# A layer pair with expert lookup: 40 instead of 20 of 64 gate batches beside the u tiles, and their work spread over the engines

## What is computed

```
top_v, top_i = top_k(sub_scores, 16)               # two halves, 128 keys each
cand = top_v[0, :, None] + top_v[1, None, :]       # 256 pairs
best_v, best_pos = top_k(cand, 16)
expert = (top_i[0] * 128 + top_i[1]) at best_pos
gates = softmax(best_v)
hid = gelu(u[expert] . h) * gates                  # 8 x 16 = 128 experts a token
out = sum over the 128 experts of hid * v[expert]
```

## Time and profile before

| | |
|---|---|
| median of the runs | 2865.11 us |
| profiled execution: span | 2863.0 us |
| own time of the profiled execution | not given apart; the runs are 2865.05, 2865.11 and 2867.16 us, so 2.1 us or a little more lie around the span |
| TensorE busy | 2716.7 us (95%) |
| VectorE | 1595.0 us (56%) |
| ScalarE | 937.4 us (33%) |
| GpSimd | 1362.7 us (48%) |
| DMA moved | 598.85 MB, mean 209 GB/s |

### The profile page before, as it was taken

One profiled execution on the slowest core, in us unless ns is written; L12 is line 12 of the kernel. 1 busy time (PEld: TensorE's weight loads), 2 busy tenths in 40 slices (PEclk: granted clock), 3 DMA queues, 4 the chain that ended last, 5 costly groups with the idle time before them and its releaser, 6 DMA issues.

```text
span 2863.0 us, 32244 instructions
## 1 busy us (share of the span) xinstructions
PE 2716.7 (95%) x12062; PEld 2057.0 (72%) x12062; DVE 1595.0 (56%) x3064; ACT 937.4 (33%) x1684; POOL 1362.7 (48%) x1004
## 2 busy tenths in 40 slices
PE   8989999998999899999998789999999999999996
PEld 7856888776888678888777678888888864444442
DVE  1033044476314343440224757999999999756667
ACT  3275343655424333222334433111113670000001
POOL 4432444566446234444352436645446664645445
PEclk9999999999999999999999899999999999999999
DMA  5321233332244136663331035999999849999998
GB/s 164 104 58 30 74 105 92 113 102 70 102 141 145 53 93 194 206 185 123 78 105 38 30 110 205 377 409 408 409 409 385 318 146 409 409 411 409 410 409 327
DMA packets 219373, 598.85 MB, mean 209 GB/s; under 512 B 22337, under 2 KB 47314, under 8 KB 218834
## 3 DMA queue, kind: packets, MB, share of 16 engines
q1 hardware_dynamic: 135280, 300.70, 30.7%
q0 software_dynamic: 75968, 275.81, 24.9%
q10 hardware_dynamic: 7970, 20.28, 2.2%
HBM read 584.84 MB, written 7.41 MB: 207 GB/s over the span
## 4 chain that ended last, share of the span: by engine, by line
PE 72%; DMA 11%; DVE 9%; POOL 3%; ACT 2%; issue 2%; POOLq 0%; DVEq 0%; ACTq 0%; SPq 0%
PE ps L1893 14%; PE ps L1373 14%; PE ps L1374 13%; PE ps L1375 13%; DMA rows<-in_v,expert 6%; DMA rows<-in_u,expert 5%; DVE ps L2597 2%; PE ps L1882 2%; DVE rows L2583 2%; PE ps L1339 1%; POOL wlo L1148 1%; PE ps L1912 1%; PE ps L1472 1%; POOL rows L1279 1%; PE ps L1559 1%
## 5 line engine op out<-in xcount | busy, mean ns | idle before, releaser
L1148 POOL TENSOR_TENSOR wlo<-wraw,whi 128x1024 fp32r<-128x1024 f32 x258 | 627.3, 2442 | 799.5 <-ACT whi L614 709.8
L614 ACT ACTIVATE whi<-wraw 128x1024 fp32r<-128x1024 f32 x258 | 270.0, 1058 | 693.0 <-PE ps L1375 593.4
L1928 PE MATMUL ps<-stream,hg 128*128 128x512 f32 x1024 | 441.7, 594 | 7.8 <-DMA stream<-in_v 7.0
L1893 PE MATMUL ps<-haff,stream 128*128 128x256 f32 x2048 | 445.6, 379 | 2.2 <-ACT stg L1038 2.2
L1373 PE MATMUL ps<-hhi,whi 128*128 128x512 f32 x1088 | 428.4, 394 | 15.6 <-DVE hlo L2059 8.7
L1893 PEld LDWEIGHTS ps<-haff,stream 128*128 128x128 f32 x2048 | 388.0, 190 | 53.8 <-ACT stg L1038 2.4
L1375 PE MATMUL ps<-hhi,wlo 128*128 128x512 f32 x1088 | 425.5, 391 | 0.0
L1374 PE MATMUL ps<-hlo,whi 128*128 128x512 f32 x1088 | 425.3, 391 | 0.0
L1279 POOL DMA_INDIRECT rows<-in_u,expert x256 | 275.6, 1077 | 239.8 <-DVE hid L2583 122.4
L1928 PEld LDWEIGHTS ps<-stream,hg 128*128 128x128 f32 x1024 | 195.2, 191 | 253.6 <-issue 244.8
L2583 DVE CUSTOM_DVE_ANT_0 rows<-rows,h_s 128x1024 f32<-128x1024 f32 x256 | 318.4, 1247 | 83.4 <-DMA rows<-in_u,expert 83.2
(11 more groups left out here) (485 smaller groups left out, 4331.8 us busy)
## 6 DMA issues: line engine op xcount, KB each, us to landing
stream<-in_ut SPq DMA_DIRECT2D x128, 512.0 KB, 6.8
stream<-in_v SPq DMA_DIRECT2D x128, 512.0 KB, 6.8
wraw<-in_w_in SPq DMA_DIRECT2D x96, 512.0 KB, 3.6
wraw<-in_w_ada SPq DMA_DIRECT2D x48, 512.0 KB, 4.1
wraw<-in_w_gu SPq DMA_DIRECT2D x88, 256.0 KB, 3.7
wraw<-in_w_down SPq DMA_DIRECT2D x22, 512.0 KB, 3.5
decs<-acs_kept ACTq DMA_DIRECT2D x16, 512.0 KB, 3.6
wraw<-in_w_br_ssm SPq DMA_DIRECT2D x16, 512.0 KB, 3.5
```

Of the source, the lines that this page charges most:

```text
L614: act.activation(whi[:, n % WSLOTS, 0:kn, :], wraw[:, n % WSLOTS, 0:kn, :], ACT.Copy).then_inc(w_hi, 1)
L1148: pool.tensor_tensor(wlo[:, n % WSLOTS, 0:kn, :], wraw[:, n % WSLOTS, 0:kn, :], whi[:, n % WSLOTS, 0:kn, :].bitcast(F32), ALU.subtract).th ...
L1893: ins = pe.matmul(ps[:, n % 2, 0:ND], stream[j][:, k, :], haff2[:, 1, k, :], start=k == 0, stop=k == KD - 1)
L1928: ins = pe.matmul(ps[:, 2 * i + half, :], hg[:, n, P * i:P * i + P], stream[j][:, 4 * half:4 * half + 4, :], start=n == 0, stop=n == NKEYS ...
```

## The change

1. `AHEAD` is 40: batches 0 to 39 come behind u tiles 88 to 127, batches 40 to 63 in the hole. Batch b's mix comes behind row 186 + 9b/4, the first one-hot behind row 184, `scale_gates` behind row 175. TensorE transposes the gates after tile 86.
2. For ahead batches ScalarE makes the second-key one-hots: 4 squares of (column - key), with the negated keys in `slot_k`, and one Relu over 512 columns. It makes the first key for token 2 only, VectorE for tokens 0 and 1.
3. Heads of the dense tiles end on VectorE with a copy of the keys and the one-hot of the position. GpSimd multiplies (`pick_scale`) and sums in four halvings (`pick_sum`), two buffers deep. Heads of `PICKED_HEADS` weave in 7 rows (tile 2) or 6 (tile 3); two heads of tile 1 weave in 6. All 24 are done by row 163.
4. The memset is gone: `mix` copies the gates of the tiles still to come into `hg` (`tensor_copy`) and multiplies the others; `late_mix` takes only the tokens whose batches are made.
5. Blocks (u,1,0) and (u,1,1) are moved ahead of (v,0,6), so the ten rows of `PE_HOLE` are rows 2 to 11 of (v,0,7), block 17 (rows 274 to 283). The row GELUs come at earlier tiles: 28, 45, 62, 78 for heads 2 to 5.
6. Two pairs of semaphores become one each (`xd_ready` and `xe_ready`; `qin_ready` and `kout_ready`, with counts to match), in parts of the program before 1810 us. These are left out of the diff.

```diff
@@ -67,20 +67,41 @@
         order.insert(order.index(("v", 1, PEER_HEADS - 4)), ("u", 1, h))
+    for h in range(2):
+        order.remove(("u", 1, h))
+        order.insert(order.index(("v", 0, PEER_HEADS - 2)), ("u", 1, h))
...
 TOP_ORDER = [(t, h) for t in (0, 2, 3, 1) for h in range(PEER_HEADS)]
-TOP_AFTER = {**{b: b + 1 for b in range(3, 12)}, **{b: b - 2 for b in range(15, 18)}}
-AHEAD = 20
+TOP_AFTER = {18: 13, 19: 14, 20: 15}
+FIRST_HEADS = TOP_ORDER[2:3 * PEER_HEADS + 2]
+WOVEN = [8] * (PEER_HEADS - 2) + [7] * PEER_HEADS + [6] * PEER_HEADS + [6, 6]
+WOVEN_FROM = [sum(WOVEN[:n]) for n in range(len(WOVEN) + 1)]
+PICKED_HEADS = FIRST_HEADS[PEER_HEADS - 2:3 * PEER_HEADS - 2]
+AHEAD = 40
 AHEAD_FROM = NKEYS + 1 - AHEAD
-AHEAD_ROW = 199
-MIX_AFTER = divmod(AHEAD_ROW + 2 * (AHEAD - 1), TOPK)
-HOT_DVE, HOT_ACT, HOT_POOL = (0,), (1, 2), (3,)
-GELU_AT = {4: 0, 21: 1, 30: 2, 49: 3, 69: 4, 88: 5, 110: 6, 117: 7}
-HOLE = TOPK * MIX_AFTER[0] + MIX_AFTER[1] + 1
-PE_HOLE = [divmod(HOLE + r, TOPK) for r in range(TOPK)]
+AHEAD_ROW = 186
+GATES_AT = AHEAD_ROW - 11
+GELU_AT = {4: 0, 12: 1, 28: 2, 45: 3, 62: 4, 78: 5, 94: 6, 101: 7}
+def batch_row(b):
+    return AHEAD_ROW + 9 * b // 4
+def late_tokens(n):
+    return 4 * (n - AHEAD_FROM + 1)
+def after_head(n):
+    return WOVEN_FROM[n + 1] + RING + 1
+HOLE = batch_row(AHEAD - 1) + 1
+HOLE_ROWS = 10
+PE_HOLE = [divmod(HOLE + r, TOPK) for r in range(HOLE_ROWS)]
@@ -89,10 +110,22 @@
 ENDS = (0, 2, 3, 1)
-NA = 4 * AHEAD
-HOLE_HALF = {AHEAD + 3 + 5 * x // 4: x for x in range(2 * TOPK)}
-HOLE_DIAG = {AHEAD + 4 + 5 * (2 * r + 1) // 4: r + DIAGS for r in range(TOPK - DIAGS)}
-HOLE_NEXT = [AHEAD + 7 + 5 * (2 * r + 1) // 4 for r in range(14)]
+HOLE_HALF = {AHEAD + 2 + x: x for x in range(2 * HOLE_ROWS)}
+HOLE_DIAG = {AHEAD + 4 + 2 * r: r + DIAGS for r in range(HOLE_ROWS - DIAGS)}
+HOLE_NEXT = [AHEAD + 7 + 2 * r for r in range(9)]
+LOADS = {2 * TOPK + RING: (0, 1), **{after_head(PEER_HEADS - 3 + 2 * q - 2): (q,) for q in range(2, 9)}, 315: (11,)}
+PICKS = {after_head(PEER_HEADS - 2 + n) + 1: n for n in range(2 * PEER_HEADS)}
+def hot_dve(b):
+    return (0, 1) if b < AHEAD else (0,)
+def hot_act(b):
+    return (2,) if b < AHEAD else (1, 2)
+HOT_POOL = (3,)
@@ -410,8 +443,13 @@
 hid = at("hid", CONST, 9, [P, SLOTS])
+slot_k = at("slot_k", CONST, 2.5, [P, NT * AHEAD])
+key_of = [tif, at("key_odd", CONST, 6.8125, [P, 2, TOPK])]
+pick_hot = [at(f"pick_hot{n}", LOW, 4 + 2 * n, [P, 2, TOPK, TOPK]) for n in range(2)]
...
 hot_pool = at("hot_pool", CONST, 4.5, [P, POOL_HOTS, NKEYS])
+iota16 = cst[:, C_IOTA:C_IOTA + TOPK].unsqueeze(1).unsqueeze(1).to_broadcast([P, 2, TOPK, TOPK])
@@ -1078,14 +1116,20 @@
             act.wait_ge(s("mix_mm"), hots_free(b))
-        mine = hot1_of(b)
-        for m in HOT_ACT:
+        first, second = hot1_of(b), hot2_of(b)
+        if b < AHEAD:
+            for m in range(4):
+                c = 4 * b + m
+                act.activation(second[:, m, :], cst[:, C_IOTA:C_IOTA + P], ACT.Square, bias=slot_k[:, c:c + 1])
+        for m in hot_act(b):
             c = 4 * b + m
-            ins = act.activation(mine[:, m, :], cst[:, C_IOTA:C_IOTA + P], ACT.Square, bias=slot_n[:, 1, c:c + 1])
+            ins = act.activation(first[:, m, :], cst[:, C_IOTA:C_IOTA + P], ACT.Square, bias=slot_n[:, 1, c:c + 1])
         link(ins)
-        for m in HOT_ACT:
+        if b < AHEAD:
+            act.activation(second.rearrange("p m n -> p (m n)"), second.rearrange("p m n -> p (m n)"), ACT.Relu, bias=1.0, scale=-1.0)
+        for m in hot_act(b):
             c = 4 * b + m
-            ins = act.activation(mine[:, m, :], mine[:, m, :], ACT.Relu, bias=slot_t[:, 0, c:c + 1], scale=slot_n[:, 0, c:c + 1])
+            ins = act.activation(first[:, m, :], first[:, m, :], ACT.Relu, bias=slot_t[:, 0, c:c + 1], scale=slot_n[:, 0, c:c + 1])
@@ -1093,22 +1137,22 @@
             act.wait_ge(s("sc_spilled"), 64)
-        if n == 124:
-            act.wait_ge(s("head_done"), top_done(*TOP_ORDER[2 * TOP_AFTER[11] + 1]))
...
         else:
-            act.activation(ps[:, n % 2, 0:NA], ps[:, n % 2, 0:NA], ACT.Gelu)
-            act.activation(hg[:, n, NA:ND], ps[:, n % 2, NA:ND], ACT.Gelu).then_inc(s("hg_ready"), 1)
+            late = late_tokens(n)
+            act.activation(ps[:, n % 2, 0:late], ps[:, n % 2, 0:late], ACT.Gelu)
+            act.activation(hg[:, n, late:ND], ps[:, n % 2, late:ND], ACT.Gelu).then_inc(s("hg_ready"), 1)
...
             row_gelu(0, GELU_AT[n])
-        if n == 98:
+        if n == AHEAD_FROM - 5:
...
             act.wait_ge(s("slots_tr"), 1)
-            act.activation(slot_t[:].rearrange("p a t -> p (a t)"), ps[:, 2, :], ACT.Copy).then_inc(s("slots_ready"), 1)
+            act.activation(slot_t[:].rearrange("p a t -> p (a t)"), ps[:, 2, :], ACT.Copy)
+            act.activation(slot_k[:], ps[:, 3, 0:NT * AHEAD], ACT.Copy, scale=-1.0).then_inc(s("slots_ready"), 1)
@@ -1305,32 +1348,49 @@
             gather_next()
+    hot_before = {batch_row(b) + RING - 6: b for b in range(AHEAD + 2)}
+    linked = [0]
+    def link(ins):
+        linked[0] += 1
+        ins.then_inc(s("pool_step"), 1)
+        pool.wait_ge(s("pool_step"), linked[0])
+    def pick_scale(n):
+        pool.wait_ge(s("head_done"), top_done(*PICKED_HEADS[n]))
+        hot = pick_hot[n % 2]
+        link(pool.tensor_tensor(hot[:], hot[:], key_of[n % 2][:].unsqueeze(2).to_broadcast([P, 2, TOPK, TOPK]), ALU.mult))
+    def pick_sum(n):
+        t, h = PICKED_HEADS[n]
+        hot = pick_hot[n % 2]
+        for half in (8, 4, 2):
+            link(pool.tensor_tensor(hot[:, :, :, 0:half], hot[:, :, :, 0:half], hot[:, :, :, half:2 * half], ALU.add))
+        pool.tensor_tensor(pick_d[:, t - 2, :, TOPK * h:TOPK * h + TOPK].unsqueeze(3), hot[:, :, :, 0:1], hot[:, :, :, 1:2], ALU.add).then_inc(s("picked"), 1)
...
         for k in range(TOPK):
-            n = TOPK * b + k - (AHEAD_ROW + RING - 4)
-            if n == 0:
-                pool.wait_ge(s("head_done"), top_done(*TOP_ORDER[2 * TOP_AFTER[11] + 1]))
-                pool.memset(hg[:, AHEAD_FROM:NKEYS, 0:NA], 1.0).then_inc(s("late_mixed"), 1)
-                pool.wait_ge(s("slots_ready"), 1)
-            if n % 2 == 0 and 0 <= n // 2 < AHEAD + 2:
-                first_hot(n // 2)
-            if TOPK * b + k == HOLE + RING:
+            r = TOPK * b + k
+            for q in LOADS.get(r, ()):
+                load_scores(q)
+            for stage, pick in enumerate((pick_scale, pick_sum)):
+                if r - stage in PICKS:
+                    pick(PICKS[r - stage])
+            if r in hot_before:
+                if hot_before[r] == 0:
+                    pool.wait_ge(s("slots_ready"), 1)
+                first_hot(hot_before[r])
+            if r == HOLE + RING:
...
                 load_scores(10)
-            if k == RING and b == 2:
-                load_scores(0)
-                load_scores(1)
-            if k == RING:
-                if b - 1 in TOP_AFTER and TOP_AFTER[b - 1] < 11:
-                    q = TOP_AFTER[b - 1] - 4 + 2
-                    load_scores(q)
-                if b - 2 == 15:
-                    load_scores(TOP_AFTER[b - 2] - 2)
-            if TOPK * b + k == gathered[0]:
+            if r == gathered[0]:
@@ -1888,7 +1947,7 @@
         if n - 2 >= AHEAD_FROM:
-            pe.wait_ge(s("late_mixed"), n - AHEAD_FROM)
+            pe.wait_ge(s("late_mixed"), n - AHEAD_FROM - 1)
@@ -1896,6 +1955,7 @@
             pe.wait_ge(s("gates_scaled"), 1)
+            pe.wait_ge(s("picked"), 2 * PEER_HEADS)
@@ -1912,7 +1972,7 @@
     pe.wait_ge(s("hg_ready"), NKEYS)
-    pe.wait_ge(s("late_mixed"), 1 + NKEYS - AHEAD_FROM)
+    pe.wait_ge(s("late_mixed"), NKEYS - AHEAD_FROM)
@@ -2506,9 +2566,11 @@
-    iota = cst[:, C_IOTA:C_IOTA + TOPK].unsqueeze(1).unsqueeze(1).to_broadcast([P, 2, TOPK, TOPK])
-    def top_keys(t, h, between=lambda: None):
+    def top_keys(t, h, between=lambda: None, woven=0):
+        picked = PICKED_HEADS.index((t, h)) if (t, h) in PICKED_HEADS else None
+        places = [0]
@@ -2522,7 +2584,9 @@
             ins.then_inc(dve_step, 1)
-            between()
+            if places[0] < woven:
+                between()
+            places[0] += 1
@@ -2554,13 +2618,18 @@
         beside(v.tensor_scalar(bij[:, 1, :], bp[:], TOPK - 1, None, ALU.bitwise_and))
-        beside(v.tensor_tensor(onehot[:], bij[:].unsqueeze(3).to_broadcast([P, 2, TOPK, TOPK]), iota, ALU.is_equal))
+        if picked is not None:
+            if picked >= 2:
+                v.wait_ge(s("picked"), picked - 1)
+            v.tensor_copy(key_of[picked % 2][:], ti[:])
+            v.tensor_tensor(pick_hot[picked % 2][:], bij[:].unsqueeze(3).to_broadcast([P, 2, TOPK, TOPK]), iota16, ALU.is_equal).then_inc(s("head_done"), 1)
+            for _ in range(places[0], woven):
+                between()
+            return
+        beside(v.tensor_tensor(onehot[:], bij[:].unsqueeze(3).to_broadcast([P, 2, TOPK, TOPK]), iota16, ALU.is_equal))
```

(50 more changed lines are left out.)

18 lines of the change are left out of this document (8 added, 10 removed).

## The result

The changed kernel takes 2896.04 us (median of 4 runs, 2894.1 to 2897.9) against 2866.14 us (4 runs, 2865.05 to 2867.29) for the kernel before on the same chip: ratio 1.0104, 95% interval 1.009 to 1.0118. It is slower, as forecast, but by 30 us and not by 14. The profiled span is 2893.2 us, 30.2 over that of before.

What follows compares the result with a forecast made beforehand. It took TensorE, DMA and VectorE to run side by side near their limits. Terms -32.7 + 17.8 - 2.7 + 2.3 + 29 = +13.7 us on the 2863.0 us span gave 2876.7, forecast as 2879 us at the median, range 2858 to 2902.

Steps and rivals of the forecast that it cites:

- Bound and stages: Behind 1810 us, u and v parts: TensorE busy throughout, DMA full at 407 and 405 GB/s, VectorE busy 356.5 of 369.6 us.
- Hole: Between u and v tiles: 24 batches instead of 44 take 40.8 us instead of 73.5, -32.7 us.
- u tiles: Expert stage's first part: 20 more gate batches beside tiles cost 0.89 us each, +17.8 us.
- tail: After the v tiles: TensorE's 2.72 us wait for the first row goes, -2.7 us; the other 62 us stay.
- ScalarE: One-hots of ahead batches: 2.66 us of work fits by 0.6 us; table loads at two row GELUs add +2.3 us.
- The new wait: Before batch 0, behind tile 88: TensorE waits for VectorE's late rows, +29 us; DMA alone would make it 26.
- 21 + 8 = +29 us: Wait at batch 0: 21 us from VectorE's own work, 8 us from GpSimd shutting VectorE out.
- counted: VectorE's program from row 48 on, reckoned without DMA limit: done at 2139.6 us, a wait of 21 us.
- 8 taken: VectorE before batch 0: GpSimd's sums for 16 heads shut it out for 8 us, of at most 38.
- two bounds of which the larger holds: Rows before batch 0: DMA alone gives 26 us of waiting, VectorE alone 21, with GpSimd's sums 29; 29 was taken.
- the longer idle stretches behind row GELUs: Two places in the ahead batches: table loads hold TensorE about 2.0 us instead of 0.87, +2.3 us.

Runs made afterwards that it cites:

- ahead20: The changed kernel with 20 batches ahead instead of 40 and the block order and row GELUs of the kernel before; 2878.35 us, ratio 1.0043.
- mult_twice: The changed kernel with one more 512-column product a head on GpSimd, which leaves the one-hots as they are; 2903.53 us, ratio 1.0128.
- the fitted kernels: The changed kernel with 30 or 34 batches ahead, block order of before, GpSimd's product one gather later, retimed starts and row GELUs; 2863.71 and 2862.74 us.

## Why the prediction was right in sign and wrong in size

*Bound and stages.* Right: DMA full, TensorE full, VectorE close behind. *Hole, u tiles, tail, ScalarE:* within 3 us each (table above), the u tiles with the luck named above. The tail fell by 5.4 and not 2.7 us. The 28 gathers in a row are there as forecast, but the first of them comes 2.1 us behind the v tiles' end (2833.7), where before it came 6.7 us behind (2798.2), with three others in front of it. The first of the 28, in the changed kernel and in before:

```profile
2835.83 0.94 POOL L1322 DMA_INDIRECT rows<-in_v,expert  x1 [54.92 <-PE ps L1972]
```

```profile
2804.91 0.94 POOL L1279 DMA_INDIRECT rows<-in_v,expert  x1 [0.30 <-issue]
```

The forecast took off only TensorE's own wait of 2.72 us; the gathers' start, 4.6 us earlier, is most of the 5.4.

*The new wait* is the step that failed: that it comes, and through VectorE's late rows, was right, but its term, "21 + 8 = +29 us", was sized too small and measured 42.7. By its own working, in the order of VectorE's program:

| stretch | counted | changed kernel | without GpSimd's sums |
|---|---|---|---|
| first u tile to row 48 | 59.5 | 61.6 | 59.5 |
| rows 48 to 104, 8 heads with 7 rows | 112.8 | 117.9 | 115.7 |
| rows 104 to 152, 8 heads with 6 rows | 103.2 | 112.0 | 104.4 |
| rows 152 to 164, 2 full heads | 28.0 | 29.6 | 28.5 |
| row 164 to batch 0 | 25.7 | 29.8 | 29.7 |

Sums: 329.2, 350.9, 337.8; less the 308.2 us to the end of tile 88 they are 21.0, 42.7 and 29.6. Of the 13.7 us missed in this term, 5.1 are GpSimd's (13.1 measured, 8 taken; its product and sums take 59 us for 16 heads, 3.7 a head where 2.4 was reckoned) and 8.6 are in the last column. There the last line stands out, 4.0 us: after the last head no small steps lie between the rows, and v rows one behind the other come 1.39 us apart, (8.25 - 1.30) / 5 in this row of the changed kernel, not the 1.17 us counted:

```profile
2137.88 8.25 DVE L2666 SCALAR_TENSOR_TENSOR ps<-rows,wrow,ps 128x1024 f32<-128x1024 f32 x6
```

The 2.9 us of rows 48 to 104 probably go with the waits for DMA that came up, 5.1 us in that trace; the count treated VectorE and DMA as two bounds of which the larger holds, but they seem to take turns, each adding what the other doesn't have ready. That is argued from the waits; no run takes DMA's part away. What makes v rows come 1.39 us apart is open too.

But the longer idle stretches behind row GELUs, 2.3 us in the forecast and 2.0 in the trace, are worth 5.4 us with 20 ahead, where TensorE's clock falls behind them.

*What was not in the working:* how far the start could be fitted. By its own terms 14.9 us were to be had in the hole less the u tiles, if no wait took them back. With the start fitted to the rows and 34 ahead 4 us came out, and 10 with the early gates, which alone bring 3.

## What to carry to other kernels

When work is brought forward beside a stage that was hidden, count what must be ready in front of it, in the program order of the engine that makes it, and move the start until that engine just makes it; then look for the engines whose queue stops at the moved wait (here GpSimd's gathers, some 1.29 us each, paid 400 us later). Offloading from VectorE to GpSimd is worth what the steps that GpSimd holds up leave of it: here, in single traces, 3.6 us (46.3 - 42.7) of the 16.7 (46.3 - 29.6) that the moved work cost there, and nothing clear of noise in the time.

## What the runs showed of the hardware

- GpSimd's two-input product (1.28 us) holds up a VectorE step with two inputs in SBUF until it has ended (0.42 becomes 1.3 to 1.8 us, 1.21 becomes up to 2.95), not searches, nor v rows with their second input in PSUM; beside its sums a step of 16 columns with one input took 0.72 instead of 0.32 us. With twice the products the wait grew by 2.4 us.
- The same 1.88 us idle stretch of TensorE was followed by a tile at full clock in the changed kernel (3.46 us), at 0.71 in ahead20 (4.92 us), and by one of 5.14 us in mult_twice.
- With early gates, so that two row GELUs load no table, the idle stretch in front of their batches, 0.87 us in before and 1.88 in the fitted kernels, is gone.
- VectorE's additions to the same PSUM sums, one behind the other, come 1.39 us apart, each listed with 1.30.
- Up to 409 GB/s of DMA for hundreds of us, with nine gathers and four stream buffers; with 8 gathers fewer out at the start of such a stretch the tail was 11.9 us longer.
